# Ten instead of nine of the eleven FFN slabs by a seven-product scheme, with eight output pieces per group

## The chip, the cores and the metric

One core of a Trainium2 chip runs the whole program. The metric is the device time of one execution in microseconds (us), given as the median of several runs. Engines: TensorE (PE) multiplies, VectorE (DVE) and ScalarE (ACT) work element by element, GpSimd (POOL) here mostly issues transfers, SyncE (SP) issues nearly all loads.

## The reference

Two transformer-like blocks on one sequence of 256 tokens with 2048 channels, all in float32. The change touches only the feed-forward part (FFN) of the second block:

```
h   = rmsnorm_2(x, ffn_norm_g)                   # 256 x 2048
hid = h @ w_ffn_in                               # 2048 x 11264: 5632 gate columns, 5632 up columns
x   = x + (silu(gate) * up) @ w_ffn_out          # 5632 x 2048
```

Behind it comes a gate of its own: `x + sigmoid(rmsnorm_2(x) @ w_ple_gate) * (p @ w_ple)`.

## The kernel before

**Pieces.** All weights are streamed from DRAM once. The unit of the stream is a *piece*: 256 rows by 512 columns of a weight matrix (512 KB, 128 partitions by 1024 numbers). Each piece is split in two for TensorE: ScalarE makes the high copy `whi` (`split_hi`, L915, and `s_hi`, L1166), VectorE the low part `wlo`, the piece minus its high copy (`split_lo`, L1873, and `s_lo`, L2553). Both go into rings of four (`RING`), so the high copy of piece g waits until TensorE is done with piece g-4. A *full piece* multiplies both halves of the tokens: 12 matmuls of 512 columns (`piece`, L1350). All four engines walk the same list of pieces g = 0, 1, 2, ... that the class `Plan` writes out, each with the side work that the plan ties to certain g.

**FFN slabs.** 512 hidden columns are a slab; there are 11 (0 to 10). A slab needs the gate columns and the up columns (8 full pieces each), the product silu(gate) * up, its transposition (two *fills* of four transposes each, `fill`, L1781, copied out by ScalarE, L1261, and VectorE, L2670), and then its share of the output: 8 full *output pieces* (four column blocks q, two pieces each). `("out", (a, b), q, start, stop)` stands for the output pieces of the slabs a and b for the column blocks q and q+1, which share an accumulator; `out1` is that of a single slab. Each finished accumulator is added to the residual by VectorE (`out_added`, L2714).

**The seven-product scheme.** Slabs 0 and 3 are computed in the plain way. The nine others use a scheme of Strassen's kind: the activations as 2 x 2 blocks (tokens by rows), the weights too (rows by gate or up), seven products instead of eight. Each product has four *product pieces* of 6 matmuls (`s_piece`, L1684). A group's 28 product pieces, called S0 to S27 here, come in the order `S_ORDER`:

- S0 to S3: M1, weights loaded into the buffer `r1` (`load_r1`, 1 MB twice)
- S4 to S7: M2 (`b21`), S8 to S11: M7 (`seventh`), from half slots of `raw`, 512 KB each
- S12 to S15: M5, a sum of weights, loaded into `r1` over M1's (`load_fifth`)
- S16, S17, S19, S21: M6, the half load `b22` added to `r1` by VectorE (`s_sum`, two pieces ahead: `S_LEAD`)
- S18, S20, S22, S23: M3, from `b22` itself
- S24 to S27: M4, for which GpSimd adds `b21` onto `r1` **by an accumulating transfer from DRAM**, one per quarter

The last of these is quoted, since the prediction follows it. GpSimd waits until VectorE has made the low part of the M6 piece of the same quarter (`S_DMA`, L518), and ScalarE's high copy of the M4 piece waits for the landing:

```
pool.wait_ge(lo_ready, S_AT[c, before, q] + 1)                                             # L897, before = "M6"
pool.dma_start(r1[:, q], s_weights(c, what, q), accum_op=ALU.add).then_inc(sem(f"r1_added{q}"), 16)   # L898
...
elif m in S_DMA:
    r1_added(act, c, m, q)                                                                 # L1171
```

The weight sums for M5 and M7 are made in DRAM ahead of time: SP copies 1 MB, GpSimd adds 1 MB by an accumulating transfer (`add_in_dram`, L875). There are four for each group; `SUM_AT` (L466 to L468) ties each to a piece. Three groups of the same kind stand in the stage before the FFN, so `M_GROUPS` = 3.

**Groups.** `BLOCKS` lists the groups: a slab, and the full pieces that are mixed among its product pieces. `add_block` (L211) writes a full piece, then as many product pieces as bring their number to `upto`, and so on:

```
upto = max(0, min(28, t * 28 // (len(std) - (1 if c == M_GROUPS - 1 else 3))))             # L218
```

With 10 full pieces that is none behind the first, then four behind each of the next seven (S0 to S3, S4 to S7, ..., S24 to S27), and two full pieces at the end. The last group has 16 full pieces.

**Loads.** SP issues loads in the order of the piece that lets their buffer go, each after waiting for that piece's low part. M1's load of the next group is let go by S25 and S27, M2's half loads of the next group by S18, S20, S22 and S23, a pair of full pieces (1 MB) by every second full piece.

**The start of the FFN.** Slab 0's 16 full pieces come first. Beside the 8th to 18th, VectorE writes the activations out whole (`act_whole`), makes their four sums, the *forms* (`act_form`), and after ScalarE's copy the forms' low parts (`act_form_lo`, L2695), one per piece. The buffer `r1` overlaps what the forms are made from, so the first load of M1 waits for the last form (`forms_summed`, L772).

Of the kernel before, what the change touches and what calls it, by code (L numbers as in the profile page):

```python
# [87 lines left out]
M_GROUPS = len(MERGE_S)  # L88
# [2 lines left out]
    (1, [("gB", 0), ("uB", 0, 0, 0, 2)]),  # L91
    (2, [("uB", 0, 0, 2, 4), ("uA", 1), ("uB", 1)]),
    (3, [("uA", 2), ("uB", 2)]),
    (1, [("gate", 3), ("up", 3, 0, 0, 2)]),
    (2, [("up", 3, 0, 2, 8), ("out", (0, 1), 0, 0, 4)]),
    (4, [("out", (0, 1), 0, 4, 8), ("out", (0, 1), 2, 0, 6)]),
    (5, [("out", (0, 1), 2, 6, 8), ("out", (3, 2), 0)]),
    (6, [("out", (3, 2), 2), ("out", (4, 5), 0, 0, 2)]),
    (7, [("out", (4, 5), 0, 2, 8), ("out", (4, 5), 2, 0, 4)]),
    (8, [("out", (4, 5), 2, 4, 8), ("out", (6, 7), 0, 0, 6)]),  # L100
    (9, [("out", (6, 7), 0, 6, 8), ("out", (6, 7), 2)]),
    (10, [("out", (8, 9), 0), ("out", (8, 9), 2)]),
]
FILLS = [(0, 1, 0, 0, "d"), (0, 2, 0, 1, "d"), (1, 1, 1, 0, "d"), (1, 2, 1, 1, "d"), (2, 7, 3, 0, "e"), (2, 9, 3, 1, "e"),
# [18 lines left out]
class Plan:  # L123
# [87 lines left out]
    def add_block(self, c):  # L211

        std = [x for u in BLOCKS[c][1] for x in self.unit(*u)]
        done = 0
        for t, x in enumerate(std):
            self.after[c, t] = self.g
            self.add_std(x, 2)
            upto = max(0, min(28, t * 28 // (len(std) - (1 if c == M_GROUPS - 1 else 3))))  # L218
            while done < upto:
                self.add_s(c, done)  # L220
                done += 1
        assert done == 28
        self.block_end.append(self.g - 1)
# [91 lines left out]
def two_blocks_kernel(nc, A, out):  # L315
    PLAN = Plan()
# [3 lines left out]
    with ctx:  # L320
# [113 lines left out]
        ple = sb("ple", [P, T, D], at=rd)  # L434
# [389 lines left out]
        def _(pool):  # L824
# [60 lines left out]
            for i, (name, n) in enumerate(POWS):  # L885
# [436 lines left out]
        def _(pe):  # L1322
# [541 lines left out]
        def _(dve):  # L1864
# [855 lines left out]
            def between(g):  # L2720
# [130 lines left out]
```

## Time and profile before

| | us |
|---|---|
| median of 3 runs (1893.72 to 1894.42) | 1894.37 |
| the profiled execution | 1893.05 |
| its span, first to last instruction | 1891.3 |
| TensorE busy in the span | 1877.2 |
| VectorE busy | 1471.8 |
| ScalarE busy | 1140.8 |

A busy TensorE is one that has a matmul in its pipeline; matmuls of 512 columns overlap, so their single lengths (0.38 us) add up to more than the span, and their pace is read from their starts. The span and the execution differ by 1.75 us of launch and end.

### The profile page before, as it was taken

Reading aid. Unit: us, or ns where it says so; the run is one execution under the profiler, and the core shown is the slowest. Engines: PE = TensorE matmul, PEld = TensorE weight load, DVE = VectorE, ACT = ScalarE, POOL = GpSimd, SP = SyncE. Lnnn points to the kernel's source line nnn. Section 1 sums busy time; section 2 is a strip of 40 time slices with the busy share of each in tenths; the row PEclk is TensorE's granted clock in tenths of the full one; section 3 lists DMA queues with packets and bytes.
Section 4 is the critical chain, followed back from the end, with each engine's and each line's share of the span. In section 5 each row is a group of like instructions: output and inputs, shape, how many; then the busy total and the mean of one; then the engine's idle time right before and its main releaser. Section 6 shows DMA issues by size and latency. Waiting matters only on the chain.

```text
span 1891.3 us, 23371 instructions
## 1 busy us (share of the span) xinstructions
PE 1877.2 (99%) x9018; PEld 1641.9 (87%) x9018; DVE 1471.8 (78%) x1591; ACT 1140.8 (60%) x1417; POOL 130.4 (7%) x156
## 2 busy tenths in 40 slices
PE   9999999999999999999999999999999999999998
PEld 8888888888888888888888888888888888888887
DVE  6889776655666677778888657988998999898865
ACT  7556445555566556566766455666766676666553
POOL 4000011000001100000000000000000000000000
PEclk9999999999999999999999999999999999999999
DMA  9799898999989879998797886788878887987653
GB/s 392 267 284 310 274 309 272 330 347 327 309 290 312 271 269 299 321 315 278 295 313 247 330 256 239 254 311 284 276 254 320 280 271 257 327 260 249 219 188 130
DMA packets 86815, 535.95 MB, mean 283 GB/s; under 512 B 10416, under 2 KB 11184, under 8 KB 40752
## 3 DMA queue, kind: packets, MB, share of 16 engines
q1 hardware_dynamic: 72736, 458.69, 63.3%
q0 software_dynamic: 13824, 75.50, 20.6%
q8 instruction: 72, 1.18, 0.2%
q10 hardware_dynamic: 144, 0.26, 0.0%
q14 instruction: 39, 0.32, 0.0%
HBM read 529.69 MB, written 105.38 MB: 336 GB/s over the span
## 4 chain that ended last, share of the span: by engine, by line
PE 90%; DVE 5%; DMA 3%; issue 1%; ACT 1%; POOL 0%; SPq 0%; ACTq 0%; DVEq 0%; POOLq 0%
PE acc L1359 44%; PE acc L1364 22%; PE aux L1724 12%; PE aux L1728 6%; DVE wlo L2556 2%; PE aux L1338 2%; DMA ple<-in_w_ffn_in 1%; DVE wlo L1876 1%; PE aux L1431 1%; DVE ple L2551 1%; DMA ple<-in_w_in 1%; DMA raw<-summed 1%; PE aux L1805 0%; ACT whi L928 0%; ACT whi L1177 0%
## 5 line engine op out<-in xcount | busy, mean ns | idle before, releaser
L1876 DVE TENSOR_TENSOR wlo<-raw,whi 128x1024 fp32r<-128x1024 f32 x512 | 623.8, 1226 | 296.4 <-ACT whi L928 288.4
L928 ACT ACTIVATE whi<-raw 128x1024 fp32r<-128x1024 f32 x511 | 534.0, 1054 | 449.8 <-PE acc L1364 414.1
L1359 PE MATMUL acc<-whi,actA_hi 128*128 128x512 f32 x892 | 344.0, 386 | 0.7 <-ACT whi L928 0.7
L1359 PE MATMUL acc<-whi,actA_lo 128*128 128x512 f32 x892 | 339.1, 380 | 0.0
L1359 PE MATMUL acc<-whi,actB_hi 128*128 128x512 f32 x796 | 304.5, 383 | 0.2 <-DVE actB_lo L2673 0.2
L1359 PE MATMUL acc<-whi,actB_lo 128*128 128x512 f32 x796 | 301.7, 379 | 0.0
L1177 ACT ACTIVATE whi<-ple 128x1024 fp32r<-128x1024 f32 x192 | 201.0, 1055 | 139.4 <-PE acc L1364 55.6
L2556 DVE TENSOR_TENSOR wlo<-ple,whi 128x1024 fp32r<-128x1024 f32 x192 | 230.2, 1220 | 31.3 <-ACT whi L1177 28.5
L1364 PE MATMUL acc<-wlo,actA_hi 128*128 128x512 f32 x892 | 229.1, 379 | 0.0
L1364 PE MATMUL acc<-wlo,actB_hi 128*128 128x512 f32 x796 | 204.4, 379 | 0.0
L2556 DVE TENSOR_TENSOR wlo<-raw,whi 128x1024 fp32r<-128x1024 f32 x144 | 174.2, 1220 | 30.6 <-ACT whi L1177 28.9
L1359 PEld LDWEIGHTS acc<-whi,actA_hi 128*128 128x128 f32 x892 | 169.1, 190 | 25.5 <-issue 2.0
L1177 ACT ACTIVATE whi<-raw 128x1024 fp32r<-128x1024 f32 x144 | 152.0, 1055 | 64.3 <-PE acc L1364 36.5
L1364 PEld LDWEIGHTS acc<-wlo,actA_hi 128*128 128x128 f32 x892 | 168.9, 189 | 24.2
L1359 PEld LDWEIGHTS acc<-whi,actA_lo 128*128 128x128 f32 x892 | 169.2, 190 | 23.4 <-issue 0.5
L1359 PEld LDWEIGHTS acc<-whi,actB_hi 128*128 128x128 f32 x796 | 150.5, 189 | 21.6 <-DVE actB_lo L2673 1.0
L1364 PEld LDWEIGHTS acc<-wlo,actB_hi 128*128 128x128 f32 x796 | 150.4, 189 | 21.6 <-DVE wlo L1876 0.3
L1359 PEld LDWEIGHTS acc<-whi,actB_lo 128*128 128x128 f32 x796 | 150.6, 189 | 20.6
L1724 PE MATMUL aux<-whi,actB_hi 128*128 128x512 f32 x360 | 136.8, 380 | 0.8 <-ACT whi L1177 0.8
L1724 PE MATMUL aux<-whi,actB_lo 128*128 128x512 f32 x360 | 136.4, 379 | 0.0
L1728 PE MATMUL aux<-wlo,actB_hi 128*128 128x512 f32 x360 | 107.4, 380 | 0.9 <-DVE wlo L2556 0.8
L1724 PE MATMUL aux<-whi,actA_hi 128*128 128x512 f32 x216 | 83.0, 384 | 0.0
(366 smaller groups left out, 2377.0 us busy)
## 6 DMA issues: line engine op xcount, KB each, us to landing
raw<-in_w_in SPq DMA_DIRECT2D x108, 1024.0 KB, 7.3
raw<-in_w_ffn_out SPq DMA_DIRECT2D x44, 1024.0 KB, 6.9
summed<-in_w_ffn_in POOLq DMA_DIRECT2D x36, 1024.0 KB, 11.6
raw<-in_w_ffn_in SPq DMA_DIRECT2D x72, 512.0 KB, 7.9
ple<-summed SPq DMA_DIRECT2D x24, 1024.0 KB, 4.9
raw<-summed SPq DMA_DIRECT2D x48, 512.0 KB, 5.4
ple<-in_w_ffn_in SPq DMA_DIRECT2D x18, 1024.0 KB, 6.9
ple<-in_w_ffn_in POOLq DMA_DIRECT2D x36, 512.0 KB, 9.9
```

The source lines that it names most:

```text
L928: act.activation(whi[:, g % RING], raw_piece(g), ACT.Copy).then_inc(hi_ready, 1)
L1177: act.activation(whi[:, g % RING], s_source(c, m, q), ACT.Copy).then_inc(hi_ready, 1)
L1338: ins = pe.transpose(bank(u)[:, c * S + t * P:c * S + (t + 1) * P], src[:, t, (c0 + c) * P:(c0 + c + 1) * P], ident[:, :])
L1359: pe.matmul(acc2(n)[:, t, :], act[x][:, k + c, t * P:(t + 1) * P], woven(whi, g, c), start=(p == 0 and c == 0 and x == 0), stop=False)
L1364: ins = pe.matmul(acc2(n)[:, t, :], act[0][:, k + c, t * P:(t + 1) * P], woven(wlo, g, c), start=False, stop=(last and c == PK - 1))
L1431: ins = pe.matmul(bank(u)[:, c], Kp[n % 2][:, c], Qp[n % 2][:, c], start=True, stop=True)
L1724: pe.matmul(o, lhs(x, q * PK + k), woven(whi, g, k), start=(q == 0 and k == 0 and x == 0 and not onto), stop=False, skip_group_check=onto)
L1728: ins = pe.matmul(o, lhs(0, q * PK + k), woven(wlo, g, k), start=False, stop=(q == 3 and k == PK - 1), skip_group_check=onto)
L1876: dve.tensor_tensor(wlo[:, g % RING], raw_piece(g), whi[:, g % RING].bitcast(F32), ALU.subtract)\
L2551: dve.tensor_tensor(x, x, half_slot(c, S_ADDEND[m], q), ALU.add).then_inc(sem("s_sum"), 1)
L2556: dve.tensor_tensor(wlo[:, g % RING], s_source(c, m, q), whi[:, g % RING].bitcast(F32), ALU.subtract)\
```

## The change

It computes ten slabs by the seven-product scheme (slab 3 joins them) and one, slab 0, in the plain way. Slab 0 now has 12 full pieces ahead of the first group; its last four `up` pieces and its first output pieces stand inside it. Each of the groups of slabs 3 to 9 has 8 output pieces; the group of slab 1 has 8 full pieces, that of slab 2 has 4, that of slab 10 has 12, and two output slabs of slab 9 move into the tail. Two groups have a written-out table of product pieces (`S_UPTO`); the others go by the same formula, with 8 in place of 10 full pieces. The fills come at other places, some of them behind a product piece. The sums in DRAM become 52 instead of 48; the four more are tied to the pieces 3, 9, 15 and 21 of the FFN stage.

```diff
-    (1, [("gate", 3), ("up", 3, 0, 0, 2)]),
-    (2, [("up", 3, 0, 2, 8), ("out", (0, 1), 0, 0, 4)]),
-    (4, [("out", (0, 1), 0, 4, 8), ("out", (0, 1), 2, 0, 6)]),
-    (5, [("out", (0, 1), 2, 6, 8), ("out", (3, 2), 0)]),
-    (6, [("out", (3, 2), 2), ("out", (4, 5), 0, 0, 2)]),
-    (7, [("out", (4, 5), 0, 2, 8), ("out", (4, 5), 2, 0, 4)]),
-    (8, [("out", (4, 5), 2, 4, 8), ("out", (6, 7), 0, 0, 6)]),
-    (9, [("out", (6, 7), 0, 6, 8), ("out", (6, 7), 2)]),
-    (10, [("out", (8, 9), 0), ("out", (8, 9), 2)]),
+    (1, [("up", 0, 0, 4, 8), ("out1", 0, 0), ("out1", 0, 1)]),
+    (2, [("out1", 0, 2), ("out1", 0, 3)]),
+    (3, [("out", (1, 2), 0)]),
+    (4, [("out", (1, 2), 2)]),
+    (5, [("out", (3, 4), 0)]),
+    (6, [("out", (3, 4), 2)]),
+    (7, [("out", (5, 6), 0)]),
+    (8, [("out", (5, 6), 2)]),
+    (9, [("out", (7, 8), 0)]),
+    (10, [("out", (7, 8), 2), ("out1", 9, 0), ("out1", 9, 1)]),
 ]
+S_UPTO = {M_GROUPS: (0, 4, 8, 18, 21, 24, 28, 28), M_GROUPS + 1: (3, 10, 18, 28)}
+FILLS = [(0, ("s", 12), 0, 0, "e"), (0, ("s", 16), 0, 1, "e"), (1, 3, 1, 0, "e"), (1, ("s", 22), 1, 1, "e"),
+         (2, 3, 2, 0, "e"), (2, ("s", 14), 2, 1, "e"), (3, 4, 3, 0, "e"), (3, 6, 3, 1, "e"),
+         (4, 1, 4, 0, "d"), (4, 3, 4, 1, "e"), (5, 4, 5, 0, "e"), (5, 6, 5, 1, "e"),
+         (6, 1, 6, 0, "d"), (6, 3, 6, 1, "e"), (7, 4, 7, 0, "e"), (7, 6, 7, 1, "e"),
+         (8, 1, 8, 0, "d"), (8, 3, 8, 1, "e"), (9, 4, 9, 0, "e"), (9, 6, 9, 1, "e"),
+         (10, 1, 10, 0, "d"), (10, 2, 10, 1, "a")]
...
+LAST_OUT = [(9, 2), (9, 3)] + [(OUT_LAST, q) for q in range(4)]
...
-        for x in self.unit("gate", 0) + self.unit("up", 0):
+        for x in self.unit("gate", 0) + self.unit("up", 0, 0, 0, 4):
             self.add_std(x, 4)
...
-            upto = max(0, min(28, t * 28 // (len(std) - (1 if c == M_GROUPS - 1 else 3))))
+            upto = S_UPTO[c][t] if c in S_UPTO else min(28, t * 28 // (len(std) - (1 if c == M_GROUPS - 1 else 3)))
...
                 if name == "ffn":
-                    add_in_dram(len(SUM_AT))
+                    add_in_dram(len([g for g in SUM_AT if g < PLAN.g_ffn]))
```

The first number of a line of `BLOCKS` is the slab, `len(std)` the number of full pieces in the group, t their index in it. In `FILLS` the first number is the group within the FFN, the second the full piece (or the product piece) behind which TensorE transposes, the third the slab.

## Rows read from the trace of the kernel before

**Rows 1.** the page's engines (busy us, share, instructions), and the chain by engine

```profile
PE 1877.2 (99%) x9018; PEld 1641.9 (87%) x9018; DVE 1471.8 (78%) x1591; ACT 1140.8 (60%) x1417; POOL 130.4 (7%) x156
...
PE 90%; DVE 5%; DMA 3%; issue 1%; ACT 1%; POOL 0%; SPq 0%; ACTq 0%; DVEq 0%; POOLq 0%
```

**Rows 2.** TensorE's timeline in the slab-8 group: start us, length us, engine, line, operation

```profile
1596.39 0.38 PE L1359 MATMUL acc<-whi,hidT_x_hi 128*128 128x512 f32 x1
...
1598.98 0.38 PE L1724 MATMUL aux<-whi,actB_hi 128*128 128x512 f32 x1
1600.27 0.38 PE L1724 MATMUL aux<-whi,actB_hi 128*128 128x512 f32 x1
...
1618.84 0.38 PE L1724 MATMUL aux<-whi,actA_hi 128*128 128x512 f32 x1
```

**Rows 3.** by stretch: busy PE, PEld, DVE, ACT, POOL; clock, DMA share, GB/s

```profile
1564.00:1627.00 63.00, 63.00 (x299) 55.22 (x298) 57.27 (x56) 43.40 (x46) 3.45 (x4) 1.00 0.85 283
1374.00:1437.00 63.00, 63.00 (x297) 55.18 (x297) 58.52 (x56) 42.92 (x45) 3.45 (x4) 1.00 0.86 284
1124.00:1185.00 61.00, 61.00 (x288) 53.50 (x287) 46.07 (x48) 34.08 (x40) 1.52 (x2) 1.00 0.70 252
```

**Rows 4.** VectorE's timeline in the slab-8 group

```profile
1594.84 1.22 DVE L1876 TENSOR_TENSOR wlo<-raw,whi 128x1024 fp32r<-128x1024 f32 x1
1595.97 2.35 DVE L2556 TENSOR_TENSOR wlo<-ple,whi 128x1024 fp32r<-128x1024 f32 x2
```

**Rows 5.** GpSimd's timeline: first adding transfer of the slab-8, slab-5 and slab-6 groups

```profile
1597.48 0.86 POOL L898 DMA_DIRECT2D ple<-in_w_ffn_in  x1 [52.28 <-DVE wlo L2556]
...
1407.52 0.86 POOL L898 DMA_DIRECT2D ple<-in_w_ffn_in  x1 [53.83 <-DVE wlo L2556]
...
1470.12 0.86 POOL L898 DMA_DIRECT2D ple<-in_w_ffn_in  x1 [52.57 <-DVE wlo L2556]
```

**Rows 6.** ScalarE's timeline: high copies of S27 in the same three groups

```profile
1617.06 1.06 ACT L1177 ACTIVATE whi<-ple 128x1024 fp32r<-128x1024 f32 x1 [2.77 <-DMA ple<-in_w_ffn_in]
...
1426.28 1.06 ACT L1177 ACTIVATE whi<-ple 128x1024 fp32r<-128x1024 f32 x1 [2.79 <-DMA ple<-in_w_ffn_in]
...
1490.28 1.06 ACT L1177 ACTIVATE whi<-ple 128x1024 fp32r<-128x1024 f32 x1 [3.96 <-DMA ple<-in_w_ffn_in]
```

**Rows 7.** ScalarE's and TensorE's timelines: S27 of the first FFN group

```profile
1236.76 1.06 ACT L1177 ACTIVATE whi<-ple 128x1024 fp32r<-128x1024 f32 x1 [2.73 <-DMA ple<-in_w_ffn_in]
...
1237.87 0.48 PE L1724 MATMUL aux<-whi,actA_hi 128*128 128x512 f32 x1
```

**Rows 8.** DMA queues: packets, MB, share by stretch: 1600:1617, 1601:1604, 1605:1615, 1590:1597

```profile
q0 software_dynamic: 576, 2.10, 67.0%
q1 hardware_dynamic: 577, 2.15, 33.5%
...
q0 software_dynamic: 99, 0.41, 94.3%
...
q0 software_dynamic: 375, 1.39, 69.7%
...
q1 hardware_dynamic: 84, 0.27, 9.5%
```

**Rows 9.** VectorE's timeline at the last form and its low parts; TensorE's 15th piece

```profile
1166.96 1.22 DVE L2691 TENSOR_TENSOR act_forms<-act_whole,act_forms 128x1024 f32<-128x1024 f32 x1
1174.10 1.22 DVE L2698 TENSOR_TENSOR actB_lo<-act_forms,actB_hi 128x1024 fp32r<-128x1024 f32 x1
...
1175.98 0.38 PE L1359 MATMUL acc<-whi,actA_hi 128*128 128x512 f32 x1
```

**Rows 10.** DMA issues (KB, median us to landing): 1168:1176, and the page's

```profile
ple<-in_w_ffn_in SPq DMA_DIRECT2D x2, 1024.0 KB, 5.8
...
summed<-in_w_ffn_in POOLq DMA_DIRECT2D x36, 1024.0 KB, 11.6
```

**Rows 11.** ScalarE's waits by releaser: us in total, times, longest

```profile
ACT whi L1177 <- DMA raw<-summed: 13.5, 18, 4.6
```

More of the change, by code:

```diff
@@ L93 @@
     (3, [("uA", 2), ("uB", 2)]),
-    (1, [("gate", 3), ("up", 3, 0, 0, 2)]),
-    (2, [("up", 3, 0, 2, 8), ("out", (0, 1), 0, 0, 4)]),
-    (4, [("out", (0, 1), 0, 4, 8), ("out", (0, 1), 2, 0, 6)]),
-    (5, [("out", (0, 1), 2, 6, 8), ("out", (3, 2), 0)]),
-    (6, [("out", (3, 2), 2), ("out", (4, 5), 0, 0, 2)]),
-    (7, [("out", (4, 5), 0, 2, 8), ("out", (4, 5), 2, 0, 4)]),
-    (8, [("out", (4, 5), 2, 4, 8), ("out", (6, 7), 0, 0, 6)]),
-    (9, [("out", (6, 7), 0, 6, 8), ("out", (6, 7), 2)]),
-    (10, [("out", (8, 9), 0), ("out", (8, 9), 2)]),
-]
-FILLS = [(0, 1, 0, 0, "d"), (0, 2, 0, 1, "d"), (1, 1, 1, 0, "d"), (1, 2, 1, 1, "d"), (2, 7, 3, 0, "e"), (2, 9, 3, 1, "e"),
[3 rows of a table removed]
+    (1, [("up", 0, 0, 4, 8), ("out1", 0, 0), ("out1", 0, 1)]),
[8 more added lines that the diff above has]
+    (10, [("out", (7, 8), 2), ("out1", 9, 0), ("out1", 9, 1)]),
+]
+S_UPTO = {M_GROUPS: (0, 4, 8, 18, 21, 24, 28, 28), M_GROUPS + 1: (3, 10, 18, 28)}
+FILLS = [(0, ("s", 12), 0, 0, "e"), (0, ("s", 16), 0, 1, "e"), (1, 3, 1, 0, "e"), (1, ("s", 22), 1, 1, "e"),
[5 rows of a table added]
 FILLS = [(c + M_GROUPS, *x) for c, *x in FILLS]
-HID_T = {0: 0, 1: 1, 2: 1, 3: 0, 4: 0, 5: 1, 6: 0, 7: 1, 8: 0, 9: 1, 10: 2}
-HID_S = [0, 1, 0, 2, 1, 0, 2, 1, 0]
+HID_T = {j: j % 2 for j in range(10)}
+HID_T[10] = 2
+HID_S = [0, 1] * 5
 OUT_LAST = 10
+LAST_OUT = [(9, 2), (9, 3)] + [(OUT_LAST, q) for q in range(4)]
 S_GROUPS = len(BLOCKS)
@@ L154, in unit @@
     def unit(self, role, j, q=0, start=0, stop=8):
+        if role == "out1":
+            return [(role, j, q, p) for p in range(2)]
         if role == "out":
@@ L199, in plan_ffn @@
         self.pair = 0
-        tail = [("ple", 0, q, 0) for q in range(4)] + [("out1", OUT_LAST, q, p) for q in range(4) for p in range(2)]
+        tail = [("ple", 0, q, 0) for q in range(4)] + [x for j, q in LAST_OUT for x in self.unit("out1", j, q)]
         for x in tail:
@@ L248, in add_s @@
         m, q = S_ORDER[i]
-        self.s_at[c, m, q] = self.g
+        self.s_at[c, m, q] = self.after[c, ("s", i)] = self.g
         self.ffn.append(("s", self.g, c, i, m, q))
@@ L1824, in _ @@
                     n, role, j, q, p = x
-                    if role == "out":
+                    if role in ("out", "out1"):
                         out_piece(n, role, j, q, p)
@@ L2727, in between @@
                 for (role, j, q), n in PLAN.ffn_slab.items():
-                    if role == "out" and g == SLABS[n][-1] + (2 if SLABS[n][-1] in PLAN.block_end else 3):
+                    if (role == "out" or role == "out1" and j != OUT_LAST) and g == SLABS[n][-1] + (2 if SLABS[n][-1] in PLAN.block_end else 3):
                         out_added(n, q)
@@ L2778, in _ @@
                 for (r, j, x), m in PLAN.ffn_slab.items():
-                    if r == "out1" and g == SLABS[m][-1] + 2:
+                    if r == "out1" and j == OUT_LAST and g == SLABS[m][-1] + 2:
                         add_slab(m, x)
```

3 rows, old and new, of the table FILLS are left out of this document.

## The prediction

> **What bounds the kernel now.** Of the page I read the engines and the chain of waits [rows 1]: TensorE is busy 1877.2 of 1891.3 us and is 90% of the chain; its granted clock in the FFN is 1.00 [rows 3]. What TensorE is given or spared is therefore the time, and so is every moment in which it waits for a piece.
>
> Its pace I read from the timeline of one FFN group, the seventh of nine (slab 8) [rows 2]. A full piece starts at 1596.39 and the next piece at 1598.98: 2.59 us for 12 matmuls. A product piece starts at 1598.98 and the next at 1600.27: 1.29, or 1.295 as half of 2.59. From the start of S16 to that of S27 it takes 19.86 (1598.98 to 1618.84): 11 product pieces, 2 full ones, and 0.43 for a fill (four transposes). So a group of before is 28 x 1.295 + 10 x 2.59 + 2 x 0.43 = 63.0 us.
>
> Beside it, the other engines in the stretch of that group and of the busiest one [rows 3]: VectorE 57.3 to 58.5 of 63 us, ScalarE 43, the DMA engines 0.85 to 0.86. Nothing is late there on average, but a little more work per time would be felt.
>
> Last I looked for the wait with least to spare. It is the M4 pieces, S24 to S27: GpSimd's four adding transfers make their weights, and may start only when VectorE has made the low part of M6's pieces (S16, S17, S19, S21), because they write over M6's source. In the slab-8 group the low part of S16 begins at 1595.97 and ends at 1597.19 [rows 4]; the first transfer is issued at 1597.48, 0.29 later [rows 5]; the fourth has landed when ScalarE's high copy of S27 starts, at 1617.06, after 2.77 us of waiting for it [rows 6]. From the first issue to the last landing that is Q = 19.6 us. Of the eight FFN groups that have 10 full pieces, those with the shortest and the longest Q give 1426.28 - 1407.52 = 18.8 and 1490.28 - 1470.12 = 20.2 [rows 5, 6]. The high copy then needs 1.11 until TensorE can start: in the first FFN group it starts at 1236.76, and TensorE starts S27 at 1237.87, at once [rows 7]. TensorE had come to its end there, so that group has no slack. In the slab-8 group S27 starts at 1618.84, 0.67 after it could.
>
> **The change, term by term.** The sums are made on the profiled execution (1893.05 us, span 1891.3); the median of the runs is 1894.37, 1.3 more.
>
> *Matmuls.* One slab goes from 16 full pieces to 28 product pieces: 192 matmuls less, 168 more, 24 x 0.216 [rows 2] = **-5.2 us**. The output pieces stay 88 (8 + 64 + 8 in the groups and the tail, 8 for slab 10), the fills 22.
>
> *The order inside a group.* The groups of slabs 3 to 9 have 8 full pieces in place of 10, and the formula t*28//(8-3) puts 0, 5, 11, 16, 22, 28 product pieces behind them where t*28//7 put 0, 4, 8, and so on. From the start of S16 to that of S27 TensorE now has 11 product pieces and **one** full piece (the one behind S21): 11 x 1.295 + 2.59 = 16.8 us. Before it had two and a fill, 19.86 [rows 2].
>
> The lead of VectorE over TensorE at S16 shrinks too. Before, the low part is done 1.79 ahead (1597.19 to 1598.98). A high copy waits for the piece four back. Counted from the end of the full piece behind which S11 to S15 now stand, VectorE does the low part of S14, a sum, S15, a sum, the full piece and S16, in steps of 1.13 (1594.84 to 1595.97 [rows 4]), after a first high copy of 1.1: 1.1 + 5 x 1.13 + 1.22 = 8.0. TensorE is at S16 after 5 x 1.295 + 2.59 = 9.07. Lead 1.0; in every second group, where a fill stands behind that full piece and its two copies of half a piece's size (half a step each, an estimate) go first, about 0.3. Mean 0.65.
>
> So from the end of S16's low part TensorE arrives at S27 after 17.5 us. What it waits for takes 0.29 + Q + 1.11. Q isn't set by the issues but by the queue. In 1600 to 1617 the adding transfers take 67.0% of the 16 engines for 2.10 MB, SP's queue 33.5% for 2.15 MB [rows 8]: 11.4 us of all engines for the four. In the three microseconds in which they have the engines to themselves they move 0.41 MB, no faster than the 1.39 MB in the ten us beside SP's queue [rows 8]. What SP's queue carries beside them stays about the same: M2's four half loads and M1's load of the next group, and a pair of output pieces, each let go by a low part between S18 and S25.
>
> Bounds for Q: from below 2.9 (issue at 1597.48 to the first packets at about 1600.4) + 11.4 = 14.3, if nothing else were on the engines; from above 20.2. I take 18.8, the shortest row, since no 1 MB load stands just ahead of the first transfer any more (the full piece before S16 now is one that frees no pair). Wait per group: 0.29 + 18.8 + 1.11 - 17.5 = **2.7 us** (0 to 4.1), in seven groups **+18.9**. TensorE has nothing to do in it: S27 is next in its order, and full pieces stand behind it.
>
> The Trainium skill would have this otherwise: its page "DMA: Bandwidth & Descriptors", section "Anatomy of one DMA — SWDGE (gpsimd) path", fits a DMA issued by GpSimd by 2.0 us plus bytes over 436 GB/s, an estimate of 3.2 us for 512 KB; the wait would then be gone, and the first rival below would hold. The rows above say 9 to 11 us from issue to landing, so the trace does not agree for an adding transfer among others.
>
> *The group of slab 2* (4 full pieces, table 3, 10, 18, 28): one full piece again between S16 and S27, but S10 to S17 stand in one run. VectorE has eight lows, two sums and one addition of M2's bank in it, and is 0.4 behind at S16's start by the same counting. Then 16.4 in place of 17.5: **+3.8 us** (0 to 5.2).
>
> *The group of slab 1 and the first slab.* S0 now comes behind 14 full pieces of the stage, not 18, so at 1175.98 on the old clock [rows 9]. Its weights are let go when VectorE ends the last form (1166.96 + 1.22 = 1168.2) and take 5.8 us [rows 10]: there by 1174, the high copy by 1175.1, just in time. But the four low parts of the forms, steps of 1.13 [rows 4, 9], now stand between the low parts of S0 to S3: that of S3 ends at 1175.2 + 6 x 1.13 + 1.22 = 1183.2 at the latest, 1182.6 if S0's comes half a step sooner; TensorE wants it at 1175.98 + 3 x 1.295 + 0.86 = 1180.7. About **+2.0 us**. Bounds: 0, if S0's weights come earlier than here, and 6, since four of the sums in DRAM (1 MB each, 11.6 us to landing [rows 10]) now run between the pieces 3 and 21 of this stage, which was at 0.70 DMA share [rows 3], and can hold up the 2 MB of M1. Between its S16 and S27 stand three full pieces: no wait. The same holds for the last group (12 full pieces).
>
> *At nothing.* Four more additions of an output slab (a step of 1.13 each) on VectorE, twelve more of the half loads, the later fills and the moved fifth and sixth tail slabs: VectorE has two low parts fewer per group, 55 to 56 of 57.8 us by its busy time and less by its steps. M7's loads: S9 comes one full piece sooner after S5, which lets its load go; ScalarE waited for the sums of M5 and M7 13.5 us in 18 times [rows 11], at 0.75 each inside its lead of two to three pieces. If that cover goes, 1 us per group.
>
> **Sum.** -5.2 + 18.9 + 3.8 + 2.0 = +19.5: 1912.6 in a profiled execution, **1914** as a median.
>
> **Rivals.**
> 1. *The transfers come home in time (faster).* The queue has idle engines when S16 is done (9.5% busy from 1590 to 1597 [rows 8]), and if SP's loads come behind the four, Q falls toward 14.3. From Q = 16.1 on no group waits: -5.2 + 0 to 2 = 1889 to 1891. Against it: eight groups with 18.8 to 20.2, and loads let go at S18, S20 and S22 that lie inside. Chance 0.20.
> 2. *The DMA engines as a whole.* 0.85 x 63 = 53.6 us of work per group, 2.8 less for 1 MB (2.15 MB are 33.5% of 17 us [rows 8]): 50.8 in 57.8. If they can't be fuller than the 0.86 of [rows 3], a group takes 59.1, 1.3 more, nine groups 11, so 1894.4 - 5.2 + 11 = 1900. For it: M4's wait is a DMA wait. Against: 9.5% in an idle stretch shows the limit to be order, not volume. Chance 0.10.
> 3. *The same wait, larger*: Q of 20.2 and the first groups at their upper bounds: 7 x 4.1 + 5.2 + 6 - 5.2 = +35, 1929. Chance 0.12.
>
> **How the numbers follow.** My forecast with waits of 1.2 to 3.7 per group: 0.58. Forecast and third rival are slower by over 0.2% (3.8 us, about what a measurement of this kernel can tell from no change): 0.70, and part of the second, 0.06, makes 0.76. Faster (below 1890.6) is most of the first rival, 0.14; the rest, 0.10, is within. The range reaches from no wait at all, 1889, to 3.6 us per group and 5 in each of the first two, 1924: 1894.4 - 5.2 + 25 + 10. The forecast's own is 1903 to 1922.
>
> **What would show it.** Right: in the groups of slabs 2 to 9 the high copy of S27 stands right behind the landing of the fourth adding transfer, TensorE starts S27 1.1 after that, and 2 to 4 us are missing in front of it; S16's start to S27's takes about 19.5 us, not 16.8; TensorE's matmuls are 24 fewer. Wrong: Q below 16, or S27's copy waiting for TensorE and not for a DMA. If the loss stands in front of other product pieces, behind VectorE, or spread over the loads, the second rival or VectorE is the cause.

## The result, and the profile after

The changed kernel takes **1944.66 us** (median of 4 runs, 1943.84 to 1947.19) against 1894.05 for the kernel before: ratio 1.0271 (1.0258 to 1.0284, the 95% interval, as behind every ratio here), **+50.6 us**. The forecast was 1914, with a range of 1889 to 1924. The direction was right; the size was short by 31 us. Two executions, one of e8_all1 (2823.7 us) and one of e15_changed_again (5137.5 us), were far slower than the rest; the medians count them, the ratios don't.

The profiled execution has a span of 1941.9 us. The page's engines and its chain by engine, to be set beside [rows 1]:

```profile
PE 1889.4 (97%) x8994; PEld 1638.5 (84%) x8994; DVE 1495.7 (77%) x1616; ACT 1147.9 (59%) x1432; POOL 136.2 (7%) x164
...
PE 69%; DVE 14%; DMA 10%; issue 3%; ACT 3%; POOL 1%; SPq 0%; ACTq 0%; DVEq 0%; POOLq 0%
```

24 matmuls fewer, as forecast. But the chain now runs through TensorE for 69% and not 90%: it leaves it for VectorE and the DMA engines. TensorE's waits in the FFN (1165 to 1800 us) say where; the columns are total us, times and the longest. Before:

```profile
PE acc L1359 <- ACT whi L928: 0.2, 1, 0.2
PE acc L1359 <- DVE actB_lo L2673: 0.2, 1, 0.2
```

After:

```profile
PE aux L1732 <- ACT whi L1185: 29.4, 15, 3.2
PE aux L1736 <- DVE wlo L2564: 7.1, 11, 1.3
```

Both lines are product pieces: their high copies (ScalarE) and their low parts (VectorE). I then set every piece of the FFN against its own pace (2.59 and 1.295 us, [rows 2]). What a group takes beyond that I call its loss, in us. The fills (0.43 each, two in most groups) and the time lost at half clock (below) are in it:

| group of slab | 1 | 2 | 3 | 4 | 5 | 6 | 7 | 8 | 9 | 10 | sum |
|---|---|---|---|---|---|---|---|---|---|---|---|
| before | 2.0 | 1.4 | (none) | 0.8 | 1.0 | 1.7 | 0.8 | 1.4 | 0.9 | 1.2 | 11.2 |
| after | 17.0 | 10.7 | 7.1 | 3.4 | 6.5 | 4.3 | 7.8 | 3.3 | 5.5 | 0.9 | 66.5 |
| of it, ahead of S27 | 1.0 | 3.3 | 2.5 | 1.7 | 3.2 | 2.6 | 3.8 | 1.5 | 3.0 | 0 | 22.6 |

66.5 - 11.2 - 5.2 (matmuls) = 50.1: the table holds all but half a microsecond of the difference.

**The wait ahead of S27, as forecast.** Timelines in the slab-7 group, to be set beside [rows 2 and 4 to 6]: VectorE's low part of S16 (the first of the two), GpSimd's first and fourth adding transfer, ScalarE's high copy of S27, TensorE from the end of S26 on:

```profile
1585.47 2.35 DVE L2564 TENSOR_TENSOR wlo<-ple,whi 128x1024 fp32r<-128x1024 f32 x2
...
1586.98 0.86 POOL L906 DMA_DIRECT2D ple<-in_w_ffn_in  x1 [53.14 <-DVE wlo L2564]
...
1595.09 0.86 POOL L906 DMA_DIRECT2D ple<-in_w_ffn_in  x1 [2.62 <-DVE wlo L2564]
...
1607.86 1.06 ACT L1185 ACTIVATE whi<-ple 128x1024 fp32r<-128x1024 f32 x1 [4.01 <-DMA ple<-in_w_ffn_in]
...
1605.15 0.70 PE L1736 MATMUL aux<-wlo,actA_hi 128*128 128x512 f32 x2
1608.96 0.79 PE L1732 MATMUL aux<-whi,actA_hi 128*128 128x512 f32 x1 [3.11 <-ACT whi L1185]
1609.55 0.63 PE L1732 MATMUL aux<-whi,actA_lo 128*128 128x512 f32 x1
1609.98 0.63 PE L1732 MATMUL aux<-whi,actA_hi 128*128 128x512 f32 x1
```

The first transfer is issued 0.29 after the low part ends (1585.47 + 1.22), the fourth has landed 20.9 us after that issue, the high copy follows at once, S27 1.10 later, and TensorE stood 3.11 us.

**What follows it, not forecast.** In the last two lines a matmul comes 0.43 after the one before, not 0.216. Stretches of the changed kernel: busy time by engine, then granted clock, DMA share and GB/s:

```profile
1605.00:1609.00 4.00, 0.76 (x4) 0.34 (x3) 1.95 (x5) 1.14 (x2) 0.00 (x0) 1.00 1.03 421
1609.00:1612.40 3.40, 3.40 (x8) 2.74 (x9) 3.40 (x4) 3.40 (x5) 0.00 (x0) 0.50 0.69 234
1206.20:1209.60 3.40, 3.40 (x9) 2.68 (x9) 3.25 (x4) 3.40 (x4) 0.00 (x0) 0.50 1.00 410
1301.80:1305.20 3.40, 3.40 (x9) 2.42 (x8) 2.66 (x3) 2.02 (x4) 0.00 (x0) 0.50 0.78 287
...
1303.00:1740.00 437.00, 416.87 (x1907) 357.06 (x1906) 382.63 (x361) 283.16 (x304) 24.22 (x28) 0.99 0.83 271
```

TensorE is nearly idle from 1605 to 1609 and then has the lower of its two clock levels, 1.2 GHz, until 1612.4: 3.4 us in which half of the work is done, 1.7 us lost. There are five such stretches in the FFN (1206.2, 1301.8, 1359.8, 1482.7, 1609.0), each behind a wait, 8.5 us in all; the three stretches of [rows 3] had 1.00.

**The group of slab 1.** Timelines: VectorE at the last form and at S0's low part, SP's issue of the four M7 half loads, ScalarE's high copies of S8 to S10, GpSimd's last two sums in DRAM:

```profile
1170.74 1.22 DVE L2699 TENSOR_TENSOR act_forms<-act_whole,act_forms 128x1024 f32<-128x1024 f32 x1
...
1177.86 1.23 DVE L2564 TENSOR_TENSOR wlo<-ple,whi 128x1024 fp32r<-128x1024 f32 x1 [4.53 <-ACT whi L1185]
1179.00 1.22 DVE L2706 TENSOR_TENSOR actB_lo<-act_forms,actB_hi 128x1024 fp32r<-128x1024 f32 x1
...
1189.45 3.73 SPq L796 DMA_DIRECT2D raw<-summed  x4
...
1196.70 1.06 ACT L1185 ACTIVATE whi<-raw 128x1024 fp32r<-128x1024 f32 x1 [4.63 <-DMA raw<-summed]
1199.81 1.06 ACT L1185 ACTIVATE whi<-raw 128x1024 fp32r<-128x1024 f32 x1 [2.05 <-DMA raw<-summed]
1204.85 1.06 ACT L1185 ACTIVATE whi<-raw 128x1024 fp32r<-128x1024 f32 x1 [3.98 <-DMA raw<-summed]
...
1180.13 0.81 POOL L890 DMA_DIRECT2D summed<-in_w_ffn_in  x1 [14.72 <-PE aux L1736]
1192.36 0.81 POOL L890 DMA_DIRECT2D summed<-in_w_ffn_in  x1 [11.41 <-PE aux L1736]
```

And what was issued between 1180 and 1206 us (KB, median us to landing):

```profile
summed<-in_w_ffn_in POOLq DMA_DIRECT2D x2, 1024.0 KB, 12.0
...
raw<-summed SPq DMA_DIRECT2D x4, 512.0 KB, 11.2
```

M7's half loads need 11.2 us beside the sums (5.8 is the page's median over the whole kernel), and S8 to S12 start 8.5 us late in all, the 1.7 of the stretch from 1206.2 among it. S0 to S3 are 4.2 us late: their weights land late, and the forms' low parts stand between theirs.

**The group of slab 2.** ScalarE waits for M7 although no sum runs:

```profile
1263.73 1.06 ACT L1185 ACTIVATE whi<-raw 128x1024 fp32r<-128x1024 f32 x1 [5.06 <-DMA raw<-summed]
```

S8 starts 2.9 us late, S9 another 0.4. Behind S21, VectorE's low part makes TensorE 1.4 late.

### The profile page after: what moved, and what is told of

It reads as the page before. It is cut to its first block, busy times and chain, and to the rows that moved or that the text cites. A ratio compares the mean times of both kernels' runs of the same rounds, so it can differ in the third digit from the quotient of the medians.

```text
span 1941.9 us, 23416 instructions
## 1 busy us (share of the span) xinstructions
PE 1889.4 (97%) x8994; PEld 1638.5 (84%) x8994; DVE 1495.7 (77%) x1616; ACT 1147.9 (59%) x1432; POOL 136.2 (7%) x164
## 4 chain that ended last, share of the span: by engine, by line
PE 69%; DVE 14%; DMA 10%; issue 3%; ACT 3%; POOL 1%; SPq 0%; ACTq 0%; DVEq 0%; POOLq 0%
PE acc L1367 37%; PE acc L1372 18%; DVE wlo L2564 8%; PE aux L1732 6%; DMA ple<-in_w_ffn_in 5%; PE aux L1736 3%; DMA raw<-summed 3%; DVE ple L2559 2%; DVE wlo L1884 2%; ACT whi L1185 1%; PE aux L1346 1%; DMA raw<-in_w_in 1%; ACT whi L936 1%; PE aux L1439 1%; DMA ple<-in_w_in 0%
## 5 line engine op out<-in xcount | busy, mean ns | idle before, releaser
L1185 ACT ACTIVATE whi<-ple 128x1024 fp32r<-128x1024 f32 x208 | 216.7, 1054 | 176.7 <-DMA ple<-in_w_ffn_in 57.1
L1367 PE MATMUL acc<-whi,actA_hi 128*128 128x512 f32 x828 | 319.6, 386 | 1.0 <-ACT whi L936 1.0
L1367 PE MATMUL acc<-whi,actA_lo 128*128 128x512 f32 x828 | 314.7, 380 | 0.0
L2564 DVE TENSOR_TENSOR wlo<-ple,whi 128x1024 fp32r<-128x1024 f32 x208 | 249.3, 1220 | 45.6 <-ACT whi L1185 44.3
L1372 PE MATMUL acc<-wlo,actA_hi 128*128 128x512 f32 x828 | 212.9, 380 | 0.0
L1367 PEld LDWEIGHTS acc<-whi,actA_hi 128*128 128x128 f32 x828 | 156.9, 189 | 23.8 <-issue 2.6
L1372 PEld LDWEIGHTS acc<-wlo,actA_hi 128*128 128x128 f32 x828 | 156.8, 189 | 22.7 <-DVE wlo L1884 0.4
L1367 PEld LDWEIGHTS acc<-whi,actA_lo 128*128 128x128 f32 x828 | 157.1, 190 | 21.7 <-issue 0.5
L1732 PE MATMUL aux<-whi,actB_hi 128*128 128x512 f32 x392 | 151.1, 385 | 7.9 <-ACT whi L1185 7.9
L1732 PE MATMUL aux<-whi,actB_lo 128*128 128x512 f32 x392 | 149.3, 381 | 0.0
## 6 DMA issues: line engine op xcount, KB each, us to landing
summed<-in_w_ffn_in POOLq DMA_DIRECT2D x40, 1024.0 KB, 11.6
```

The costliest lines, as they stand in the source:

```text
L1185: act.activation(whi[:, g % RING], s_source(c, m, q), ACT.Copy).then_inc(hi_ready, 1)
L1367: pe.matmul(acc2(n)[:, t, :], act[x][:, k + c, t * P:(t + 1) * P], woven(whi, g, c), start=(p == 0 and c == 0 and x == 0), stop=False)
L1372: ins = pe.matmul(acc2(n)[:, t, :], act[0][:, k + c, t * P:(t + 1) * P], woven(wlo, g, c), start=False, stop=(last and c == PK - 1))
L1732: pe.matmul(o, lhs(x, q * PK + k), woven(whi, g, k), start=(q == 0 and k == 0 and x == 0 and not onto), stop=False, skip_group_check=onto)
L2564: dve.tensor_tensor(wlo[:, g % RING], s_source(c, m, q), whi[:, g % RING].bitcast(F32), ALU.subtract)\
```

## The experiments

All are the changed kernel with the edit shown; ratios are to the kernel before, beside which each ran on one chip.

**Who makes the wait ahead of S27.** Theory A: the four adding transfers and too little work between S16 and S27. Rival B: TensorE waits wherever it stands, since the DMA engines or VectorE are late as a whole.

e1_order:

```diff
-S_UPTO = {..., M_GROUPS + 1: (3, 10, 18, 28)}
+S_UPTO = {..., M_GROUPS + 1: (3, 10, 18, 28),
+          **{M_GROUPS + i: (0, 5, 11, 16, 19, 23, 28, 28) for i in range(2, 9)}}
```

> The changed kernel (1944.7 us) with another table of product pieces in the groups of slabs 3 to 9: (0, 5, 11, 16, 19, 23, 28, 28), so that two full pieces, not one, stand between S16 and S27. Theory A (the wait for the fourth adding transfer, as predicted): the trace of the changed kernel lost 2.45, 1.70, 3.19, 2.58, 3.78, 1.49 and 3.04 us ahead of S27 in these groups, 18.2 together, and three stretches at granted clock 0.50 stand right behind three of them (1.7 us each). With 2.6 us more for TensorE, 0 to 1 us of wait per group is left: 1922 to 1929, and Q (first issue to last landing) stays at 18.4 to 20.9. Theory B (the DMA engines as a whole are full, and the loss only changes its place): 1940 to 1946, with new waits ahead of S0 or S8.

Measured 1926.93, ratio 1.0184 (1.0160 to 1.0208), in A's range. The waits ahead of S27 in slabs 3 to 9 fall from 18.2 to 8.7 us (0.3 to 2.0 a group, more than the 0 to 1 expected), and their three stretches at half clock are gone. TensorE's waits in the FFN:

```profile
PE aux L1733 <- ACT whi L1186: 18.1, 11, 3.7
PE aux L1737 <- DVE wlo L2565: 4.8, 6, 1.1
```

e2_small:

```diff
-pool.dma_start(r1[:, q], s_weights(c, what, q), accum_op=ALU.add)...
+pool.dma_start(r1[:, q, 0:1, 0:128], s_weights(c, what, q)[:, 0:1, 0:128], accum_op=ALU.add)...
```

> The changed kernel with an eighth of each adding transfer for M4 (64 of 512 KB; the rest of M4's weights is left without its second term), in all groups. It keeps every wait and order, and takes away what the four transfers cost on the DMA engines. Theory A: no wait ahead of S27 anywhere (22.6 us in the ten groups of the FFN), no half-clock stretch behind S27 (four, 6.8 us), and about 1 us in the stage before: 1912 to 1917, and the waits of the first two groups ahead of S8 to S12 stay. Theory B (DMA engines full): these go too, 1900 to 1908. Theory C (VectorE sets the groups, the transfer is only the last to come): above 1930.

Measured 1914.61, ratio 1.0111 (1.0090 to 1.0132), 30 less than the changed kernel. No wait is left ahead of any S27:

```profile
PE aux L1732 <- ACT whi L1185: 8.6, 4, 4.4
PE aux L1736 <- DVE wlo L2564: 7.4, 17, 1.1
```

The fourth transfer still lands 13.6 to 18.3 us after the first issue, though it carries an eighth: its own issue waits for M6's low parts (8.1 to 8.7 us in slabs 3 to 9), and it then takes 6.2 to 6.9 there. The groups of slabs 1 and 2 keep losses of 15.4 and 7.6. So A holds for S27, and a second cause sits in the first two groups. Since the edit takes traffic away too, it can't exclude B by itself; the next one moves the same bytes.

e9_order4, three full pieces between S16 and S27 (its expectation and that of e7_all say four, and that of e5_spread three where e1_order has two: they count the one ahead of S16):

```diff
+          **{M_GROUPS + i: (0, 5, 11, 16, 18, 22, 26, 28) for i in range(2, 9)}}
```

> The changed kernel with one table added for slabs 3 to 9: four full pieces between S16 and S27, two instead of four between S27 and the next S0; the four DRAM sums stay by the group of slab 1. Theory (in e7_all the groups without a sum, of slabs 3, 4 and 9, lost 1.5 to 3.2 us and had no wait ahead of S27): seven groups at about 2.4 us in place of 37.9 us in all in the changed kernel, 21 us: 1944.7 less 21, 1921 to 1926. Rival (two full pieces are too few for the M1 weights, so that S0 to S3 wait 1 to 2.6 us in each group, as in slabs 5 and 7 of e7_all, whose cause was then not the sum): 1930 to 1935.

Measured 1922.51, ratio 1.0150 (1.0125 to 1.0175). The seven groups lose 15.2 us in place of 37.9, with no wait ahead of S27 and none of more than 0.4 at S0 to S3: the theory, at its whole size, and B is wrong for these groups. ScalarE's high copy of S27 in the slab-7 group again stands right behind the landing, but TensorE comes to S27 only 3.0 later:

```profile
1600.65 1.06 ACT L1186 ACTIVATE whi<-ple 128x1024 fp32r<-128x1024 f32 x1 [2.17 <-DMA ple<-in_w_ffn_in]
...
1603.63 0.38 PE L1733 MATMUL aux<-whi,actA_hi 128*128 128x512 f32 x1
```

**The half clock.** e4_warm:

```diff
+if (m, q) == ("M4", 3) and c - M_GROUPS in (1, 2, 4, 5, 6, 8):
+    pe.wait_ge(sem("s_second_row"), c + 1)
+    for _ in range(10):
+        pe.matmul(aux[:, 2, :]..., actA[0][:, 0, 0:P], actA[0][:, 0:2, :], start=True, stop=True)
```

> The changed kernel with ten matmuls of 512 columns, 2.16 us, whose results nothing reads, ahead of S27 in the six groups where TensorE waits there for more than 2.3 us (slabs 2, 3, 5, 6, 7, 9). They lie inside the wait. Theory E (TensorE's idle time ahead of S27 is what takes the clock down behind it): no stretch at granted clock 0.50 behind S27, where the changed kernel has four (at 1301.8, 1359.8, 1482.7 and 1609.0), 1.7 us each: 1937 to 1940. Rival (the stretches come from something else, or the matmuls only push S27 back): 1944 or more, stretches as before.

Measured 1941.17, ratio 1.0247 (1.0227 to 1.0267), between the two expectations: some 4 less by the ratios, at the edge of what runs tell apart, where four stretches are 6.8. All stretches at half clock in the six groups with the extra matmuls are gone; the only one behind an S27 is in slab 4, which has no extra matmuls. Slab 1 has two stretches in this profile and one in that of the changed kernel.

**The group of slab 1.** Theory D: the DRAM sums make M7's loads late. e3_nosums leaves the four new ones out; the last group reads the sums of the group before it:

```diff
-SUM_AT += [... for i in range(4 * S_GROUPS - len(SUM_AT))]
+SUM_AT += [... for i in range(4 * (S_GROUPS - 1) - len(SUM_AT))]
...
```

> The changed kernel without the four weight sums in DRAM that came new into the start of the FFN (the last group reads the sums of the group before it, so its M5 and M7 use other weights). Theory D: these 8 MB hold up the loads of M7 in the group of slab 1, where 7.2 us are lost ahead of S8 to S12 with a half-clock stretch in it (1.7 of them), and M1's first load (0.9): 1934 to 1937, and the low parts of the forms still cost 2 to 4 us ahead of S1 to S3. Rival: the run of ten product pieces behind the third full piece is what VectorE and ScalarE cannot follow: 1943 to 1946, and the same waits stay.

Measured 1940.62 (1934.05 to 1943.18), ratio 1.0240 (1.0216 to 1.0264), between the two expectations. The slab-1 group loses 7.5 in place of 17.0, so D is right there; but the profiled execution, 1943.18, has 27 us at half clock where the changed kernel has 17, and the other groups lose 9.1 more. In that execution the gain was given back.

e5_spread keeps the sums, one each in the groups of slabs 5 to 8, with the order of e1_order:

```diff
...
-SUM_AT += [PLAN.g_out + 11 + 6 * i for i in range(4 * S_GROUPS - len(SUM_AT))]
+SUM_AT += [PLAN.g_out + 11 + 6 * i for i in range(4)] + [S_AT[M_GROUPS + 4 + i, "M1", 0] for i in range(4)]
```

> The order of e1_order (three full pieces between S16 and S27, two of them ahead of S24) for slabs 3 to 9, and the four new DRAM sums one each in the groups of slabs 5 to 8 instead of all by the group of slab 1. Theory D (the sums sit on the DMA queues that carry the M7 and M5 loads of the group of slab 1, and cost that group about 8 us): e1_order's 1926.9 less 7 to 9, 1917 to 1921. Rival (what the sums leave is taken back by the waits ahead of S27, as in the profiled execution of e3_nosums, or by the sums' own traffic in the groups of slabs 5 to 8): 1924 to 1929, with S27 waits in slabs 5 to 8 larger than in slabs 3, 4 and 9.

Measured 1944.10, ratio 1.0266 (1.0250 to 1.0282): some 16 worse than e1_order by the ratios, and worse than the rival's 1924 to 1929. It isn't S27: these four groups lose 33.5 us (e1_order: 9.8), and 23.1 of them stand ahead of S8 to S10, five stretches at half clock (8.5) included. ScalarE's copy of S8 in the slab-5 group, and the DMA queues and issues of 1422 to 1445:

```profile
1439.11 1.06 ACT L1186 ACTIVATE whi<-raw 128x1024 fp32r<-128x1024 f32 x1 [7.82 <-DMA raw<-summed]
```

```profile
q1 hardware_dynamic: 1200, 5.94, 68.0%
q0 software_dynamic: 144, 1.05, 22.4%
...
ple<-summed SPq DMA_DIRECT2D x2, 1024.0 KB, 12.1
raw<-summed SPq DMA_DIRECT2D x4, 512.0 KB, 10.8
...
summed<-in_w_ffn_in POOLq DMA_DIRECT2D x1, 1024.0 KB, 12.6
```

The same part of the group in e1_order (1428 to 1451), where no sum runs:

```profile
q1 hardware_dynamic: 1485, 7.14, 89.0%
...
ple<-summed SPq DMA_DIRECT2D x2, 1024.0 KB, 5.5
raw<-summed SPq DMA_DIRECT2D x4, 512.0 KB, 5.6
```

One sum (1 MB) doubles the time of the loads beside it and costs each of the four groups about 6 us (33.5 - 9.8 over four), 2.1 of them at half clock. It takes 22.4% of the 23 us for 1.05 MB, 5.2 us of all 16 engines; SP's queue moves 1 MB in 2.6 (68.0% for 5.94 MB). The Trainium skill, page "DMA: Bandwidth & Descriptors", section "Queues, rings and completion order", says that each DMA engine takes its queues in turn, a packet from each; the two blocks above fit that, SP's loads going from 5.6 to 10.8 us beside one more queue, but no row shows the order of the packets.

e7_all and e8_all1 add e6_first (below) to e5_spread, e7_all with the order of e9_order4:

> All three edits (first two groups six and six, sums spread, and an order for slabs 3 to 9 with four full pieces between S16 and S27, which leaves two instead of three between S27 and the next S0). Theory (the losses are separate and add): 1926.9 less 8 (sums) less 7 (first groups) less 6 (what e1_order left ahead of S27): 1903 to 1909. Rival (two full pieces, 5.2 us, are too few for the M1 weights, whose load took 5.8 us): waits ahead of S0 or S2 of 1 to 2 us a group take the place of those ahead of S27: 1911 to 1920.

> As e7_all, with the order of e1_order for slabs 3 to 9 (three full pieces between S27 and the next S0). Theory (the losses add): 1926.9 less 8 less 7: 1909 to 1914. Rival (the spread sums cost the groups of slabs 5 to 8 what they leave in that of slab 1): 1918 to 1923.

Measured 1936.89, ratio 1.0227 (1.0208 to 1.0245), and 1945.64, ratio 1.0269 (1.0250 to 1.0288): both above their rivals' ranges too. The four groups with a sum lose 29.5 and 32.6 us, as in e5_spread. The waits right ahead of S0 that e7_all has in slabs 5 and 7 (2.2 and 1.3 us) are not M1's: there a fill waits for VectorE's product silu(gate) * up (3.1 us in two waits). e9_order4, without spread sums, has none of them.

e10_early makes the four sums before the FFN, where the DMA engines had time left:

```diff
-SUM_STEP = 5.2
+SUM_STEP = 4.8
-SUM_AT += [199 + int(5.4 * i) for i in (0, 1, 2, 3, 8, 9, 10, 11, 12, 13)]
+SUM_AT += [199 + int(5.4 * i) for i in (0, 1, 2, 3, 4, 7, 8, 9, 10, 11, 12, 13)]
```

> The changed kernel with all DRAM sums made ahead of the stage before the FFN: 25 instead of 23 in the first stage, and two more where the DMA engines stood at 0.71 and 0.49 of their time (around 650 and 690 us); the last four of the list again fall where those of the kernel before fell. Theory (a 1 MB sum costs nothing where DMA time is left, and 7 to 9 us in all beside the M7 loads of the group of slab 1): M7 waits of that group gone but the last (1.3 us), 1935 to 1938. Rival (the four sums cost where they are put, as in e5_spread, or the waits ahead of S27 take it back, as in e3_nosums): 1940 to 1946.

Measured 1943.58, ratio 1.0254 (1.0236 to 1.0272), the rival's number, though the slab-1 group loses 7.5 and not 17.0. So it was run again beside the changed kernel, and with ten matmuls as in e4_warm ahead of S27 in slabs 2 to 9 (in seven of these eight groups, not in slab 8's, e10_early had fallen to half clock behind S27):

> e10_early unchanged, beside the changed kernel on the same chip. If the sums' removal is worth what it measured there: 1 to 2 us faster than the changed kernel. If e10_early or the changed kernel fell on an unlucky run: 6 to 9 us faster.

> The changed kernel itself, once more, for its own spread from run to run: 1942 to 1947 expected from its first four runs.

> e10_early with ten unread matmuls (2.16 us) ahead of S27 in the groups of slabs 2 to 9, the eight in which the granted clock of e10_early fell to half behind S27. Theory G (what e10_early won in the group of slab 1 was given back at half clock: eight stretches at 1.7 us against four in the changed kernel): 8 x 1.7 = 13.6 less in the profiled kernel, 1928 to 1933, and no stretch at half clock behind S27. Rival (the time given back is the longer wait for the adding transfers alone, with the clock a companion; the weights landing sets S27's start, and the time after it is made up elsewhere): 1938 to 1943.

Measured: e14_early_again 1935.41, ratio 1.0229 (1.0211 to 1.0248); e15_changed_again 1947.11, ratio 1.0278 (1.0264 to 1.0291); e13_early_warm 1930.34, ratio 1.0191 (1.0178 to 1.0205). The stretch 1303 to 1740 of e10_early, of e14_early_again and of e13_early_warm (the figure behind POOL's is the clock):

```profile
1303.00:1740.00 437.00, 413.76 (x1870) 353.44 (x1870) 376.05 (x353) 278.03 (x298) 24.16 (x28) 0.97 0.82 266
```

```profile
1303.00:1740.00 437.00, 417.67 (x1902) 357.66 (x1902) 381.23 (x358) 281.31 (x302) 24.16 (x28) 0.98 0.83 271
```

```profile
1303.00:1740.00 437.00, 432.92 (x2006) 371.87 (x2005) 388.23 (x365) 285.56 (x307) 24.16 (x28) 1.00 0.84 274
```

The same program differs from run to run by its time at half clock: three runs of e14_early_again took 1934.1 to 1935.5 at a mean granted clock of 0.993 to 0.995, the fourth 1944.9 at 0.989. A mean lower by 0.005 is 1% of the time at half clock, some 19 us, that is 10 us of work. With the extra matmuls the four runs lie within 1928.0 to 1932.4, in theory G's range. The sums by the group of slab 1 cost 8 to 12 us: 11.7 on one chip (1947.1 to 1935.4), 10.6 by the ratios of e4_warm and e13_early_warm, 8.3 between e9_order4 and e11_both below. What hid that in e10_early was the clock, but not alone: its profile has eight stretches of 3.4 us where that of the changed kernel has five (5.1 us more lost), and its waits ahead of S27 are 26.5 us in place of 22.6. In e3_nosums it is eight stretches and 25.3 us. Beside e14_early_again, on the same chip, the extra matmuls are worth 5 us and not the 13.6 expected from e10_early's profile.

**The first two groups.** e6_first:

```diff
-(1, [("up", 0, 0, 4, 8), ("out1", 0, 0), ("out1", 0, 1)]),
-(2, [("out1", 0, 2), ("out1", 0, 3)]),
+(1, [("up", 0, 0, 4, 8), ("out1", 0, 0)]),
+(2, [("out1", 0, 1), ("out1", 0, 2), ("out1", 0, 3)]),
...
-S_UPTO = {M_GROUPS: (0, 4, 8, 18, 21, 24, 28, 28), M_GROUPS + 1: (3, 10, 18, 28)}
+S_UPTO = {M_GROUPS: (0, 2, 6, 18, 23, 28), M_GROUPS + 1: (0, 3, 6, 18, 23, 28)}
-FILLS = [..., (1, 3, 1, 0, "e"), ...
+FILLS = [..., (1, ("s", 14), 1, 0, "e"), ...
```

> The first two groups alone are changed: two full pieces move from the group of slab 1 to that of slab 2 (six and six instead of eight and four), and a full piece stands between S4 and S8 and between S1 and S4 in both; all the rest as in the changed kernel. Theory F (in these two groups the loads of M1 and M7 weights are late because too few full pieces stand between a buffer's release and its next use): S0 to S3 of slab 1 4.2 us to about 2, S7 to S8 of slab 2 3.3 to about 0.5, S1 to S2 0.6 to 0, the wait ahead of S27 in slab 2 3.3 to about 1.5; the DRAM sums keep the M7 loads of slab 1 late: 1935 to 1939. Rival (the same full pieces only move the loss to where they were taken): 1943 to 1947.

Measured 1950.70, ratio 1.0289 (1.0262 to 1.0317): above the rival's range too, and by the ratios no better than the changed kernel. Slab 2 loses 10.1 in place of 10.7, slab 1 19.0 in place of 17.0.

**Together.**

> e9_order4 and e10_early together. Theory (separate losses, so they add): 1912 to 1918. Rival (one takes back what the other gives, as e5_spread did): 1920 to 1928.

e11_both (e9_order4 and e10_early): 1914.22, ratio 1.0106 (1.0083 to 1.0128), in the theory's range. With S27 in time in slabs 3 to 9 nothing there gives the sums' gain back, and the two add: 22 and 8 less.

e12_all, besides:

```diff
-M_GROUPS + 1: (3, 10, 18, 28)
+M_GROUPS + 1: (3, 7, 18, 28)
```

> e11_both, and in the group of slab 2 the second full piece between S6 and S7 instead of ahead of S3, so that one stands between S4 and S8. Theory (the M7 load is late there since its buffer came free only four product pieces before S8): S7 to S8 from 2.5 us to under 0.5 and no half-clock stretch behind it: e11_both less 2 to 4. Rival (the loss only moves, as in e6_first): e11_both within 1.

Measured 1911.19 (1910.07 to 1911.39), ratio 1.0086 (1.0071 to 1.0101), 3.0 less than e11_both (1910.87 to 1919.29), which these runs don't tell from nothing. S8 of slab 2 is in time, as the theory says; but the group keeps 10.7 us, as the rival says, now by waits for the adding transfers (0.8 and 2.5 ahead of S26 and S27) and VectorE (2.8). TensorE's waits in the FFN of e12_all:

```profile
PE aux L1737 <- DVE wlo L2565: 6.4, 8, 1.3
PE aux L1733 <- ACT whi L1186: 3.9, 5, 1.8
```

It is the best found, some 34 us better than the change as made and 16 us slower than the kernel before. Its groups lose 33.4 us, 18.5 of them in slabs 1 and 2, against 11.2 before.

## Why the prediction was right or wrong

*Matmuls, -5.2*: right, 24 fewer.

Of the 31 us by which the size was short, 13 are in slab 1 (17.0 less 2.0 before and 2.0 forecast), 5.5 in slab 2 (10.7 less 1.4 and 3.8), and 12 in the other groups (38.8 less 7.8 and 18.9; 5.1 of them at half clock behind three waits, 4.0 behind VectorE).

*The wait ahead of S27, +18.9*: right in mechanism, and in size partly by luck. Seven groups wait 18.2 us. Q is 18.4 to 20.9, mean 19.4, where 18.8 was taken, which alone would make 23 us; but TensorE came to S21 late in six of the seven groups, 4.0 us in all (*VectorE* below), and had that much less to wait for at S27. VectorE leads by 0.2 to 1.2, mean 0.7, as forecast. The wait falls to nothing with smaller transfers (e2_small) or more work ahead of it (e9_order4). The 9 to 11 us for one transfer stand in none of the prediction's rows; the page of the kernel before has a median of 9.9.

*The group of slab 2, +3.8*: the wait ahead of its S27 is 3.3, right. But the step looked only at S16 to S27. The table (3, 10, 18, 28) puts S3 to S9 in one run, so that S8 comes four product pieces after the release of its buffer, and what the prediction put *at nothing* for M7's loads failed: 3.3 us, seen in the changed kernel's trace, and e12_all, which puts a full piece between, has S8 in time.

*The group of slab 1, +2.0 (0 to 6)*: **the step that failed most.** It had the sums in DRAM as a risk to M1's load alone. They held up M7's: 17.0 us of loss, 9.5 of which go with the sums (e3_nosums, e10_early). The 11.6 us of [rows 10] were read as a latency; a sum also takes a share of the DMA engines from SP's loads. S0 to S3 come 4.2 us late and not 2.0: VectorE's last form ends at 1172.0 and not at the forecast 1168.2, and M1's weights land at 1176.8 and 1179.3. The group also waits 1.0 ahead of its S27, where the prediction had no wait.

*Left out*: **the clock.** A wait of 3 us was priced at 3 us; five of the changed kernel's waits are each followed by a stretch at 1.2 GHz, 1.7 us more each (8.5 us), eight in e15_changed_again's profile. The Trainium skill's page "TensorE: Matmul & The Clock Gate", section "HAM oscillation — how this bites in real kernels", describes a clock that falls behind each wait for a DMA; the trace agrees in part, since the 2.6 and 3.0 us ahead of S27 in slabs 6 and 9 were followed by 1.00, the 2.5 in slab 3 by 0.50.

*VectorE at nothing*: TensorE comes late behind it by 1.9 us in slab 1, 1.6 in slab 2, 0.4 to 0.8 in most of the others, behind S16, S20 or S21, where the product pieces now stand in runs. Part of it only shortens the wait ahead of S27: with the order of e1_order it vanishes in slabs 3 to 9 together with part of that wait.

*Rivals.* The first (in time) is wrong. The third (the same wait, larger) is wrong in its Q, 20.2, and its upper bounds for slabs 1 and 2, 6 and 5.2, were both passed (15.0 and 9.3 more than before). The second (DMA engines as a whole) is wrong for slabs 3 to 9: with another order, and the same bytes, they run at 58.2 to 60.4 us a group (e9_order4), 57.0 being the pieces alone. In slab 1, and in the groups where e5_spread put a sum, it is near the truth: there what else was on the DMA engines set most of the loss.

*Open*: why Q differs by 2 us from group to group, and which wait is followed by half clock. No version was found that keeps the 5.2 us of matmuls: slabs 1 and 2 have 12 full pieces between them, and e6_first and e12_all only moved part of their loss.

## What to carry to other kernels

When pieces are taken out of an order, look at every wait that they covered, not at the tightest alone: for each load, count the work between its buffer's release and its use. A transfer put "where there is time" costs what it does to the loads beside it, so read landing times with and without it. And price a wait of a few microseconds in front of TensorE with the clock behind it: a loss may hide a gain elsewhere until the waits are gone.

## What the runs showed of the hardware

- GpSimd's adding transfer of 512 KB lands 6 to 13 us after its issue. With an eighth of the bytes (e2_small) the first two of each group land after 2.7 to 3.2 us, but the fourth of slabs 3 to 9 only after 6.2 to 6.9, and its issue comes 8.1 to 8.7 us after the first.
- One 1 MB sum beside SP's loads: 512 KB loads from 5.6 to 10.8 us at about the same total (312 and 305 GB/s). The sum took twice the engine time of SP's loads for a byte (4.9 and 2.6 us of all 16 engines per MB).
- Ten matmuls without use (2.16 us) ahead of a wait kept the clock at 1.00 behind it in each of the six and eight groups where they were tried. The runs of e13_early_warm lie 4.4 us apart, those of e14_early_again 10.8; those of e4_warm, 7.0 apart, are no closer than the changed kernel's 3.3.
